# Paired attention: the exponentials turned against a diagonal of the sums' reciprocals

## The reference

```
s = jnp.where(valid, s + bias[:, None, None], NEG_INF)
m = jnp.max(s, axis=-1, keepdims=True)
p = jnp.exp(s - m)
den = jnp.sum(p, axis=-1, keepdims=True)
o = jnp.einsum('bhrnqk,bhrnkd->bhrnqd', (p / den).astype(v.dtype), vb)
```

## Time and profile before

| | |
|---|---|
| median of three runs | 3334.12 us (3332.98 to 3334.88) |
| span of the profiled execution (its own time is not listed apart from it) | 3332.6 us |
| PE busy | 3122.0 us, 94% of the span |
| DVE busy | 977.3 us, 29% |
| ACT busy | 468.7 us, 14% |
| POOL busy | 175.7 us, 5% |
| mean granted TensorE clock | 0.963 of full speed |
| first stage, from its first score product to the next block | 117.6 to 149.1 us |
| second stage | 824.4 to 872.6 us |
| third stage | 1803.8 to 1843.2 us |

### The profile page before, as it was taken

One profiled execution on the slowest core, in us unless ns is written; L12 is line 12 of the kernel. 1 busy time (PEld: TensorE's weight loads), 2 busy tenths in 40 slices (PEclk: granted clock), 3 DMA queues, 4 the chain that ended last, 5 costly groups with the idle time before them and its releaser, 6 DMA issues. The chain is left out here.

```text
span 3332.6 us, 37240 instructions
## 1 busy us (share of the span) xinstructions
PE 3122.0 (94%) x15401; PEld 1836.2 (55%) x15401; DVE 977.3 (29%) x2009; ACT 468.7 (14%) x993; POOL 175.7 (5%) x210
## 2 busy tenths in 40 slices
PE   8999999798898999999798886999999999999998
PEld 6588888344685644644443775444444444444444
DVE  2422785366642366200365433000000000000001
ACT  1301000231421100000232212000000000101000
POOL 0000000000340000000001420000000000000000
PEclk9999999899998999889898997999999999999999
DMA  7243765112101255212223002989898888898885
GB/s 229 89 145 130 245 224 202 57 61 84 21 3 63 94 206 174 69 57 82 80 76 78 3 2 84 322 272 297 270 294 272 298 269 299 268 300 268 285 281 172
DMA packets 291966, 560.56 MB, mean 168 GB/s; under 512 B 28240, under 2 KB 40908, under 8 KB 291834
## 3 DMA queue, kind: packets, MB, share of 16 engines
q1 hardware_dynamic: 270755, 497.71, 45.4%
q0 software_dynamic: 13856, 53.11, 4.4%
q10 hardware_dynamic: 7223, 7.85, 0.8%
HBM read 557.42 MB, written 1.23 MB: 168 GB/s over the span
## 5 line engine op out<-in xcount | busy, mean ns | idle before, releaser
L1262 PE MATMUL bank<-normed,weight_ring 128*128 128x256 f32 (+2 forms) x2528 | 674.7, 428 | 13.0 <-PEq L2145 7.9
L1262 PEld LDWEIGHTS bank<-normed,weight_ring 128*128 128x128 f32 x2528 | 458.0, 192 | 221.3 <-issue 182.4
L2608 PE MATMUL bank<-weight_ring,work 128*128 128x512 f32 x1024 | 449.4, 593 | 10.1 <-ACT work L2641 10.1
L2608 PE MATMUL bank<-work 128*128 128x512 f32 x768 | 337.5, 592 | 0.0
L2608 PEld LDWEIGHTS bank<-weight_ring,work 128*128 128x128 f32 x1024 | 192.0, 190 | 241.1 <-issue 241.1
L656 PE MATMUL bank<-normed,weight_ring 128*128 128x512 f32 (+1 forms) x704 | 281.2, 560 | 24.7 <-PEq L1357 24.7
L1262 PE MATMUL bank<-work,weight_ring 128*128 128x256 f32 (+2 forms) x928 | 285.5, 467 | 12.2 <-PEq L1228 12.2
L2662 DVE TENSOR_TENSOR work<-bank,work 128x512 f32<-128x512 f32 x56 | 38.7, 692 | 789.1 <-PE bank L2608 789.1
L217 DVE SCALAR_TENSOR_TENSOR work<-work,small 128x512 f32<-128x512 f32 x336 | 237.6, 749 | 22.5 <-DMA work<-in_mod_w 15.7
L2608 PEld LDWEIGHTS bank<-work 128*128 128x128 f32 x768 | 144.7, 190 | 176.0 <-issue 176.0
L1262 PEld LDWEIGHTS bank<-work,weight_ring 128*128 128x128 f32 x928 | 177.3, 193 | 116.5 <-issue 102.0
(11 more groups left out here) (341 smaller groups left out, 2601.2 us busy)
## 6 DMA issues: line engine op xcount, KB each, us to landing
weight_ring<-in_moe_w_gate SPq DMA_DIRECT2D x64, 1024.0 KB, 5.1
weight_ring<-in_moe_w_up SPq DMA_DIRECT2D x64, 1024.0 KB, 5.1
weight_ring<-in_moe_w_down SPq DMA_DIRECT2D x64, 1024.0 KB, 5.0
work<-in_mod_w POOLq DMA_DIRECT2D x48, 1024.0 KB, 6.4
work<-in_moe_w_gate SPq DMA_DIRECT2D x48, 1024.0 KB, 5.1
work<-in_moe_w_up SPq DMA_DIRECT2D x48, 1024.0 KB, 5.1
work<-in_moe_w_down SPq DMA_DIRECT2D x48, 1024.0 KB, 5.1
weight_ring<-in_w_in SPq DMA_DIRECT2D x36, 1024.0 KB, 5.1
```

What stands on the lines that cost most here:

```text
L1262: last = nc.tensor.matmul(banks(gi)[j][:, to], w[:, k, j * P:(j + 1) * P], a, start=k0 + k == 0, stop=k0 + k == total - 1)
L2608: last = nc.tensor.matmul(self.bank[b], xg[:, kk], w[:, k], start=kk == 0, stop=kk == DT - 1)
```

## The change

The exponentials stay as they are. In place of the keys-wide product (L1507), DVE multiplies the identity matrix with the column of reciprocals, which gives a diagonal matrix of 128x128 (`diag`, six buffers). In place of the transpose (L1455), PE takes a plain product with the exponentials as stationary and the diagonal as moving operand: the result is the transposed exponentials with each query's column scaled. The values and all later steps are the same. DVE's write of a diagonal waits until the buffer's last reader has finished. The number and order of the instructions on every engine's list stay the same.

```
+        diag = self.arena.take("diag", 6, P)
...
-                            last = nc.tensor.transpose(PT[h][:, t * P:(t + 1) * P], pr[:, i % 6, t * P:(t + 1) * P], ident)
+                            last = nc.tensor.matmul(PT[h][:, t * P:(t + 1) * P], pr[:, i % 6, t * P:(t + 1) * P], diag[:, i % 6], start=True, stop=True)
...
-                        e = pr[:, i % 6, 0:pairs[p]["keys"]]
-                        nc.vector.tensor_scalar(e, e, st[:, i % 6, 2:3], None, ALU.mult).then_inc(probs_ready.sem, 1)
+                        if i >= 6:
+                            dve.wait_ge(turned.sem, turned.at(i - 5))
+                        nc.vector.tensor_scalar(diag[:, i % 6], ident, st[:, i % 6, 2:3], None, ALU.mult).then_inc(probs_ready.sem, 1)
```

More of the change, by code:

```diff
@@ L1559, in head_attention @@
             windowed.advance(2 * len(pair_in))
-        self.arena.free("pr", "pt", "st")
+        self.arena.free("pr", "pt", "st", "diag")
     def attention(self, units):
```

## The result

The change makes the kernel slower: 3347.43 us (median of four runs, 3346.94 to 3350.61) against 3333.88 us for the kernel before, measured beside it, a ratio of 1.0044 with a 95% interval of 1.0030 to 1.0058. That is 13.6 us where 21.6 were forecast. A second set of runs gave 3347.54 against 3333.17 (1.0039, 1.0025 to 1.0053).

What follows compares the result with a forecast made beforehand. PE was taken as the bound, DVE right behind. Added PE time of 25.8 us less waits of 0.6, 2.6, 0.6 and 0.4 gave 21.6, added to 3334.1: 3355.7 us, range 3350 to 3363.

Steps and rivals of the forecast that it cites:

- What bounds the kernel: All three attention stages: PE sets the pace, 1.81 us per pair with 256 keys and 3.11 with 512.
- Two records for a tile, 0.111 us each: At PE's turn: a plain product takes two passes, adding 0.115 us per tile, 25.8 us in all.
- Nothing for VectorE's shorter product: VectorE's product in the stages: 10.1 us of its time saved, bringing only what PE waits for it.
- What comes off PE's waits: PE's waits at the turn: 0.6 us off in the first stage, 2.6 in the second, 0.6 and 0.4 in the third.
- the third stage's first turn: Start of the third stage: turn grows by about 1.8 us, partly absorbed by a wait, +0.5 instead of 0.9.
- No other stage changes: Outside the three attention stages: no change in time, as weight transfers run ahead of PE before and after.
- The reference point: Whole kernel: 21.6 us, a difference on the 3332.6 us span, added to the runs' median of 3334.1 us.
- The chances: Whole kernel: forecast 0.70, waits stay 0.13, clock 0.09, PE not the bound 0.05, fourfold product 0.03.
- the cases named as slower: Whole-kernel time: forecast, waits staying, clock rising sooner and fourfold product, together given 0.94 for slower.
- the clock rises sooner: Rival, start of the second stage: more turn work ends the 1.2 GHz stretch earlier, giving back 4.3 us: 3351.4; chance 0.09.

Runs made afterwards that it cites:

- VectorE's half alone: Changed kernel with PE's turn put back to the plain transpose with the identity, VectorE still making diagonals, division left out: 3329.13 us against 3333.17, ratio 0.9982.
- PE's half alone: Kernel before with the transpose replaced by a plain product with the identity, VectorE's keys-wide product kept: 3348.09 us against 3333.17, ratio 1.0039.
- third_only: Kernel before with the change applied in the third attention call only: 3336.86 us against 3333.41, ratio 1.0012.
- fill_third_13: Kernel before with 13 idle plain products of 256 columns (5.5 us) behind the third stage's last mix only: 3335.87 us against 3333.41, ratio 1.0010.
- after: First profile of the changed kernel, whole change against the kernel before: median 3347.43 us against 3333.88, ratio 1.0044; profiled span 3345.1 us.
- the two copies of the changed kernel: Whole change against the kernel before, the changed kernel profiled again twice without further edits: 3347.54 us and 3348.8 us.

## Why the prediction was wrong

- **What bounds the kernel**: right. PE sets the pace with 256 and with 512 keys. VectorE's half alone left 1.81 us where it was, and PE's half alone gave the whole 2.31 us.
- **Two records for a tile, 0.111 us each**: right. 448 records; (1.98 - 1.09) / 8 is 0.111 us. What the sum missed is that the fixed part of a turn grew too: 1.09 - 8 * 0.111 = 0.20 us instead of 0.16. A tile costs 0.125 us (256 keys) and 0.12 us (512 keys) in steady state, not 0.115, and the 224 tiles 96 * 0.125 + 128 * 0.12 = 27.4 us, not 25.8.
- **Nothing for VectorE's shorter product**: right by PE's half alone.
- **What comes off PE's waits**: right in kind, too small. The rows of waits are gone as forecast, and by PE's slower pace, as PE's half and VectorE's half show; GpSimd still stretches VectorE's product and it no longer matters. But of the 27.4 us only 20.0 appear in the stages of the first profile (18.7 to 19.9 over the three of the change, against the mean of 119.3 us of before), so about 7.4 us were covered and not 4.2. The first stage grew by 6.8 (forecast 6.8), the second by 7.8 (8.4), the third by 5.5 (6.4). Part of it is the third stage's first turn, which I let cost 0.5 us net and which cost 0.1: it grew by 1.12 us and not by 1.8, as the clock rose within it. Another part is that I took only PE's own wait rows; in the last pairs of the first stage, where no scores are left, the turns of two pairs lie 145.24 - 143.84 = 1.40 us apart before and 149.37 - 147.69 = 1.68 after, 0.28 more instead of 0.5. PE's timeline there, before and then after:

```profile
143.84 0.66 PE L1455 MATMUL bank<-tables,work 128*128 128x128 f32 x4
...
145.24 0.90 PE L1455 MATMUL bank<-tables,work 128*128 128x128 f32 x4 [0.16 <-DVE work L1507]
```

```profile
147.69 1.16 PE L1456 MATMUL bank<-work 128*128 128x128 f32 x8
...
149.37 1.16 PE L1456 MATMUL bank<-work 128*128 128x128 f32 x8
```

  Before, PE had been waiting for VectorE at that place.
- **"No other stage changes"**: this is the step that failed; without it the sum of 19.5 us in the stages would have given 3353.4 us, within the range. It was argued from the transfers and not from the clock. With the change the program regains 1.9 us behind the third stage, because 3.4 us at 1.2 GHz do not occur there; third_only and fill_third_13 show that it hangs on the third stage. It regains 2 to 4 us more between the second and the third stage in each of the three profiles of the change, again with a higher granted clock; that this is due to the change is not shown.
- **The reference point**: adding a difference to the median was sound, but the difference of two single profiles, 12.5 us, hides that executions of one kernel differ by about 2 us outside the stages (3211.0 to 3213.4 for before, 3205.9 to 3207.8 for the change).
- **The chances**: the cases named as slower add up to 0.95, not 0.94; nothing hangs on it.

Together: forecast 21.6; the stages 20.0 at most and 19.5 on the mean of the profiles (138.8 against 119.3); less 1.9 behind the third stage and about 3.0 between the second and the third on the means, 14.6. The medians say 13.6 and 14.4.

No kernel of these beats before and computes the whole result: VectorE's half alone is 4.0 us faster, but its result lacks the division, so it is no candidate.

The rival "the clock rises sooner" was the nearest to what happened, with 3351.4 us. It had the place wrong: it looked at the start of the second stage only, where in `after` the first 9.2 us stayed slow as before (9.1). In the two copies of the changed kernel it was 6.7 us, and their second stage is 1.1 us shorter; but fill_third_13, whose second stage is the old one, has 6.7 us too, so this is no work of the change.

## What to carry to other kernels

In these traces a float32 transpose on PE is one record and the plain product of the same tile is two of the same length, so folding a scaling into the transpose pays only where PE has room for the second pass; count the records of both kinds in the trace before trading an elementwise operation for it. Where the pace is PE's, a shorter operation on another engine is worth only the waits that it removes, and half of a change alone, each way, shows that in two runs. When PE's busy pattern changes, look at the granted clock behind the changed part too: untouched instructions can gain or lose a few microseconds there, and a filler of idle products tells whether the change's own instructions are needed for it. Before giving a reason for such a shift, compare what the engine did in front of it in a profile with it and one without.

## What the runs showed of the hardware

- Turning one 128x128 float32 tile took 0.1075 us as a transpose (weight load 141 ns) and 2 * 0.111 us as a plain product (weight load 192 ns), all at 2.4 GHz.
- Going from one shape of product to another costs about 0.16 us on PE beside the products, and 0.20 us at the turn of plain products (worked out from 0.59 and 1.02 us, and from 1.09 and 1.98 us, for 4 and 8 tiles).
- VectorE's product that fell under GpSimd's addition took 1.31 us with 128 columns and 1.17 us with 256 columns in the earlier trace rows, against 0.29 and 0.35 elsewhere: in these two instances the hold-up did not shrink with the operation.
- Code that was not changed became faster behind the third stage by 1.9 us, most of it within 20 us (granted clock 0.91 and 1.00), and in a stretch of 68.6 us by 3.3 or 4.9 us (41.0, 34.1 or 30.7 us of it at 1.2 GHz).
- The clock fell behind the third stage in `before` and did not in third_only, although PE had done the same in the 7.4 us ahead of the fall (158 records, 4.42 and 4.43 us busy).
